# Two heads of a pair on the two halves of the partitions in the delta stage, and x loaded transposed

## Chip, cores and metric

The kernel runs on one core of a Trainium2 chip. The metric is device time in microseconds (us) from the first to the last instruction of the program; one launch computes the whole layer. The engines are named as in the profile: PE is TensorE's matmuls, PEld its weight loads, DVE is VectorE, ACT is ScalarE, POOL is GpSimd, SP is the engine that issues nearly all DMAs.

## What is computed

One layer of a streaming encoder over 4096 prompt frames and 8 running streams of 16 frames, all in float32. The part that the change touches is this, cut from the reference:

```python
xn = rms_norm(h, ln_g)            # h: 4096 x 1024;  xn = h * rsqrt(mean(h*h)) * ln_g
proj = xn @ w_in                  # columns: q,k,v of group A (1536), a, b, z_A, q_B, k_B, v_B, z_B
conv = silu(depthwise_conv4(qkv_a))                       # per channel, along the frames
q, k = l2_norm(q) * 64**-0.5, l2_norm(k)                  # 8 heads of 64
# gated delta rule in blocks of 64 frames; decay, kk, qk, u, w: solved ahead of the scan
def step(s, xs):                                          # 64 blocks, one after the other
    u_c, w_c, qk_c, qd_c, kt_c, gt_c = xs
    v_new = u_c - w_c @ s
    o_c = qd_c @ s + qk_c @ v_new
    s = s * gt_c + kt_c.T @ v_new                         # the state carries the recurrence
    return s, o_c
o_a = rms_norm(o_a, gdn_norm_g) * silu(z_a)
y = x + concat(o_a, o_b) @ w_out, and then a gated embedding on top
```

## The kernel before

The program is a row of stages with a barrier of all engines between them: `project_a`, `project_b`, `delta`, `delta_sample`, `attend_sample`, `attend`, `combine`. Each engine has its own instruction stream, written out by hand; the streams meet at semaphores only, and an engine that waits holds everything behind it in its own stream.

**project_a** makes q, k, v of group A with the channels on the partitions. The work is 16 blocks of 256 frames (the middle one holds the sample tile too), each with 12 groups of 128 channels. Every product is three float32r matmuls (high x high, low x high, high x low; `matmul3`, lines 88 to 90) for each of 8 slices of the contraction, 24 matmuls a group. While block b is multiplied, the tiles of 128 frames of block b+1 are made ready, two of them (33 in all). A tile goes: SP loads x (`load_x`, L276, two buffers), ACT squares and sums (`square`, L442), POOL makes 1/rms (`norm`), ACT scales x in place (`scale`, L446), PE turns it with 8 transposes into two PSUM banks (`transposes`, L560, called after groups 3 and 8), DVE multiplies by ln_g on the way out (`full`, L662), ACT rounds to the high part (`split_hi`, L453), DVE subtracts for the low part (`split_lo`, L668), SP spills the turned tile for project_b (`spill`, L280). In every group ACT takes the product out of PSUM (`a_raw`, L513), DVE does the four taps of the convolution (L682, L685), ACT the SiLU. Keys and queries of the last block are multiplied after groups 0 to 3 (L600), and small steps for the gates are spread over the groups (`gate_steps`). Block b+1 may start when the low part of its last tile is there. The weights are split once at the start: 32 pieces, `hi_part` on ACT, `lo_part` on DVE for even pieces and on POOL for odd ones.

**project_b** reads the spilled tiles and splits its own weights in the same way (ACT L1228, DVE L1314); meanwhile the engines solve the triangular systems and write per-chunk matrices `UQ`, key rows `krow`, `ketr` and query factors `qrow`.

**delta** runs the recurrence: 64 chunks n of 64 frames, two to a tile t of 128 frames. Rows are frames: the even chunk of a tile sits on partitions 0 to 63, the odd one on 64 to 127, and the eight heads lie side by side in the columns. A chunk is a chain through three engines, cut into two halves x of four heads so that they can follow one another:

- PE `keys_state(n, x)` (L1738): keys times state S, into `psS`
- DVE `residual` (L1829): r = value - gain x that, one instruction for each head on 64x64
- PE `solved` (L1757): the solved matrix times r, into `psV`
- ACT `new_values` (L1673): out of PSUM, 64x256 for each half
- PE `new_state` (L1774): scaled keys times new values, into `psD`
- DVE `state` (L1841): S = decayed S + `psD`; then the next chunk's keys_state

Beside it PE does `queries_state` (L1749) and, one chunk late, `outputs(n - 1)` (L1765); ACT does `decayed` (L1693), `out_rows` (L1680), `out_square` (L1686), and `values(t + 1)` (L1664) at the end of odd chunks; DVE does `keys(t + 1)` (L1813) and `out_sums` (L1847); POOL scales the queries (`scaled`, L1624) and norms the outputs. After the even chunk PE turns keys and values of the next tile in one call of eight transposes (`prepare`, L1721 and L1723). Each 64x64 product is two matmul instructions in the profile. Before the first chunk, SP brings `rows` (three kinds of factors, 24 rows), PE turns them in 32 transposes (L1781), and DVE copies them.

Of the kernel before, what the change touches and what calls it, by code (L numbers as in the profile page):

```python
# [31 lines left out]
P = 128  # L32
# [82 lines left out]
def project_a(nc, d, s):  # L115
# [13 lines left out]
    RING, SLOTS = 6, 7  # L129
# [4 lines left out]
    with ExitStack() as stack:  # L134
# [3 lines left out]
        x_raw = [ph.sb(f"a_x{i}", [P, D]) for i in range(2)]  # L138
        squares = ph.sb("a_squares", [P, D], mybir.dt.bfloat16)
        x_full = [ph.sb(f"a_x_full{i}", [P, KT, P]) for i in range(2)]  # L140
# [30 lines left out]
        psT = ph.ps("a_psT", [P, KT * P])  # L171
# [16 lines left out]
        x_in = [ph.sem(f"a_x_in{i}") for i in range(2)]  # L188
# [3 lines left out]
        scaled = ph.sem("a_scaled")  # L192
        xT_ps = ph.sem("a_xT_ps")
# [19 lines left out]
        spilled = [ph.sem(f"a_spilled{i}") for i in range(2)]  # L213
# [48 lines left out]
        def lo_part(eng, m, done):  # L262
            k, a, b = PIECES[m]
            eng.wait_ge(w_hi_ok, m + 1)
            eng.tensor_tensor(w_lo[:, k, a:b], stage[m % SLOTS][:, 0:b - a], w_hi[:, k, a:b].bitcast(F32),
                              ALU.subtract).then_inc(done, 1)
# [4 lines left out]
        def _(sp):  # L271
            def load_x(t):
                if t >= 2:
                    sp.wait_ge(xT_ps, t - 1)
                src = d.x_p[order[t] * P:(order[t] + 1) * P, :] if t != SAMPLE else d.x_s
                sp.dma_start(x_raw[t % 2][:, :], src).then_inc(x_in[t % 2], 16)  # L276

            def spill(t):
                sp.wait_ge(full_ok, t + 1)
                sp.dma_start(d.xT[order[t]], x_full[t % 2][:, :, :]).then_inc(spilled[t % 2], 16)  # L280
# [36 lines left out]
            load_x(0)  # L317
            with nc.allow_non_contiguous_dma(reason="small per-channel constants, once"):
                sp.dma_start(lnT[:, :], d.ln_g.rearrange("(k p) -> p k", p=P)).then_inc(ln_in, 16)
            load_x(1)  # L320
            for m, (k, a, b) in enumerate(PIECES):
# [5 lines left out]
                if m == 5:  # L327
                    with nc.allow_non_contiguous_dma(reason="small per-channel constants, once"):
# [4 lines left out]
                        sp.dma_start(alog[0:HA, :], d.a_log.rearrange("(h o) -> h o", o=1)).then_inc(consts, 16)  # L333
                if m == 16:
                    load_x(2)
                    spill(0)
                if m == 20:
                    load_x(3)
                    spill(1)
            for b in range(BLOCKS):  # L340
# [27 lines left out]
            for i in range(2):  # L368
                sp.wait_ge(stored[i], 16 * (BLOCKS // 2))
                sp.wait_ge(kq_out[i], 32 * 2 * BLOCKS)  # L370
                sp.wait_ge(spilled[i], 16 * ((TILES + 1 - i) // 2))
# [7 lines left out]
        def _(pool):  # L379
# [36 lines left out]

            norm(0)
            norm(1)
            for i in range(HALVES // 2):
                lo_part(pool, 2 * i + 1, w_lo_g)  # L420
            for b in range(BLOCKS):
# [15 lines left out]
        def _(e):  # L437
            def square(t):
                e.wait_ge(x_in[t % 2], 16 * (t // 2 + 1))
                if t:  # L440
                    e.wait_ge(ssq_ok, t)
                e.activation(squares[:, :], x_raw[t % 2][:, :], ACT.Square, accum_out=ssq[:, t % 2:t % 2 + 1]).then_inc(ssq_ok, 1)  # L442

            def scale(t):
                e.wait_ge(rstd_ok, t + 1)
                e.activation(x_raw[t % 2][:, :], x_raw[t % 2][:, :], ACT.Copy, scale=rstd[:, t % 2:t % 2 + 1]).then_inc(scaled, 1)  # L446

            def split_hi(t):
# [4 lines left out]
                e.activation(xT_hi[b % 2][:, :, a * P:(a + 1) * P], x_full[t % 2][:, :, :], ACT.Copy).then_inc(hi_ok, 1)  # L453

            def hi_part(m):
                k, a, b = PIECES[m]
                e.wait_ge(w_in[m % SLOTS], 16 * (m // SLOTS + 1))
                e.activation(w_hi[:, k, a:b], stage[m % SLOTS][:, 0:b - a], ACT.Copy).then_inc(w_hi_ok, 1)
# [19 lines left out]
            square(1)  # L478
            scale(0)
            hi_part(0)  # L480
            hi_part(1)
            scale(1)
            for m in range(2, HALVES):
# [3 lines left out]
                if m == 8:  # L487
# [13 lines left out]
            for b in range(BLOCKS):  # L501
                ahead = list(tiles_of(b + 1))
                for g in range(G):
# [19 lines left out]
                    if ahead:  # L523
                        if g == 0:
                            square(ahead[0])
                        if g == 1:
                            scale(ahead[0])
                        if g == 4:
                            split_hi(ahead[0])
                    if len(ahead) > 1:  # L530
                        if g == 5:
                            square(ahead[1])
                        if g == 6:
                            scale(ahead[1])
                        if g == 9:
                            split_hi(ahead[1])
                    if len(ahead) > 2:
                        if g == 7:
                            square(ahead[2])
                        if g == 9:  # L540
                            scale(ahead[2])
# [10 lines left out]
        def _(pe):  # L552
            pe.wait_ge(filled, 7)

            def transposes(t):
                pe.wait_ge(scaled, t + 1)
                if t:
                    pe.wait_ge(full_ok, t)
                for k in range(KT):
# [3193 lines left out]
```

## Time and profile before

| | us |
|---|---|
| median of 3 runs | 3620.63 (3614.67 to 3621.94) |
| time of the profiled execution | 3616.96 |
| its span | 3615.2 |
| PE busy in it | 3311.5 |
| DVE, ACT, POOL busy | 2440.0, 1519.8, 1348.5 |
| mean granted clock of TensorE | 0.965 of full |

The span is cut into stages by the instructions that belong to each: project_a to 783, project_b to 1721, delta to 2057, the sample stages to 2260, attend to 2760, combine to the end. A matmul is listed from its issue to its modelled end and overlaps the next ones, so the distance from one start to the next, not the listed duration, is what it costs.

### The profile page before, as it was taken

The numbers are of one execution on the slowest core, as the hardware profiler recorded it, in microseconds if no ns is written. First come the engines' busy times: TensorE is split into PE (matmuls) and PEld (weight loads), VectorE is DVE, ScalarE is ACT, GpSimd is POOL, SyncE is SP. The second block draws the span as 40 slices with busy tenths as digits, with TensorE's granted clock in tenths as the row PEclk, the third lists the DMA queues.
The fourth block names the chain that finished last, engine by engine and source line by source line (L and its number), as shares of the span: only waits on it lengthen the run. The fifth ranks groups of instructions, "written<-read, shape, count | busy, mean of one in ns | idle before, by whom it ended". The sixth has DMA issues, their size and how long they took to land. (4 is left out here: it accounts for less than half of the span.)

```text
span 3615.2 us, 68943 instructions
## 1 busy us (share of the span) xinstructions
PE 3311.5 (92%) x26156; PEld 2827.1 (78%) x26156; DVE 2440.0 (67%) x4770; ACT 1519.8 (42%) x2959; POOL 1348.5 (37%) x1561
## 2 busy tenths in 40 slices
PE   7999999969998999999777667999997999999998
PEld 6999899957886888888676544888885788778887
DVE  7777687745997878682465454766666655666765
ACT  5555455533223323211455423666664222344443
POOL 3222222219896836310466610000001233455664
PEclk9999999989999999999799878999998999999999
DMA  5343244344436552523866355222223544322221
GB/s 157 109 112 113 86 118 114 100 146 132 135 104 184 173 152 103 147 79 113 254 212 228 81 146 187 89 74 75 88 74 129 186 155 148 112 76 100 79 105 63
DMA packets 330646, 455.19 MB, mean 126 GB/s; under 512 B 189555, under 2 KB 212371, under 8 KB 325702
## 3 DMA queue, kind: packets, MB, share of 16 engines
q1 hardware_dynamic: 330318, 450.77, 39.5%
q8 instruction: 211, 3.46, 0.4%
q14 instruction: 117, 0.96, 0.1%
HBM read 276.56 MB, written 176.76 MB: 125 GB/s over the span
## 5 line engine op out<-in xcount | busy, mean ns | idle before, releaser
L88 PE MATMUL b_psP<-b_w_hi,b_xT_hi 128*128 128x512 f32 x1320 | 519.2, 393 | 41.2 <-DVE b_xT_lo L1319 24.3
L89 PE MATMUL b_psP<-b_w_lo,b_xT_hi 128*128 128x512 f32 x1320 | 517.1, 392 | 0.0
L90 PE MATMUL b_psP<-b_w_hi,b_xT_lo 128*128 128x512 f32 x1320 | 516.6, 391 | 0.0
L88 PE MATMUL a_psG<-a_xT_hi,a_w_hi 128*128 128x256 f32 (+1 forms) x1536 | 454.0, 296 | 21.1 <-DVE a_xT_lo L668 19.5
L89 PE MATMUL a_psG<-a_xT_lo,a_w_hi 128*128 128x256 f32 (+1 forms) x1536 | 441.5, 287 | 0.0
L90 PE MATMUL a_psG<-a_xT_hi,a_w_lo 128*128 128x256 f32 (+1 forms) x1536 | 441.0, 287 | 0.0
L88 PE MATMUL h_psM<-h_w_hi,h_c_hi 128*128 128x512 f32 x928 | 371.1, 400 | 37.8 <-DVE h_w_lo L3257 16.3
L89 PE MATMUL h_psM<-h_w_lo,h_c_hi 128*128 128x512 f32 x928 | 366.3, 395 | 0.0
L90 PE MATMUL h_psM<-h_w_hi,h_c_lo 128*128 128x512 f32 x928 | 366.1, 394 | 0.0
L3241 POOL TENSOR_TENSOR h_c_lo<-h_c_lo_whole,h_c_hi 128x512 fp32r<-128x512 f32 x162 | 219.2, 1380 | 325.0 <-ACT h_c_hi L3342 325.0
L88 PEld LDWEIGHTS a_psG<-a_xT_hi,a_w_hi 128*128 128x128 f32 x1536 | 295.3, 192 | 42.7 <-DVE a_xT_lo L668 23.5
L88 PEld LDWEIGHTS b_psP<-b_w_hi,b_xT_hi 128*128 128x128 f32 x1320 | 249.8, 189 | 99.7 <-DVE b_xT_lo L1319 48.0
L685 DVE SCALAR_TENSOR_TENSOR a_act<-a_raw,a_taps,a_act 128x256 f32<-128x256 f32 x576 | 289.1, 502 | 20.6
L89 PEld LDWEIGHTS a_psG<-a_xT_lo,a_w_hi 128*128 128x128 f32 x1536 | 295.7, 192 | 0.0
L90 PEld LDWEIGHTS a_psG<-a_xT_hi,a_w_lo 128*128 128x128 f32 x1536 | 295.5, 192 | 0.0
L90 PEld LDWEIGHTS b_psP<-b_w_hi,b_xT_lo 128*128 128x128 f32 x1320 | 249.7, 189 | 52.4
L3540 DVE TENSOR_TENSOR h_acc<-h_acc,h_psM 128x512 f32<-128x512 f32 x322 | 210.0, 682 | 119.7 <-PE h_psM L90 119.6
L89 PEld LDWEIGHTS b_psP<-b_w_lo,b_xT_hi 128*128 128x128 f32 x1320 | 250.1, 189 | 51.4
L408 POOL COPY a_halo<-a_raw 128x3 f32<-128x3 f32 x192 | 74.3, 387 | 503.3 <-ACT a_raw L513 501.9
L2652 DVE CUSTOM_DVE_ANT_0 f_neg<-f_score,f_bias 128x640 f32<-128x640 f32 (+4 forms) x256 | 192.4, 780 | 82.4 <-PE f_score L2552 52.7
L88 PEld LDWEIGHTS h_psM<-h_w_hi,h_c_hi 128*128 128x128 f32 x928 | 177.3, 191 | 80.0 <-issue 33.4
L1282 ACT ACTIVATE b_rows<-b_psP 128x512 f32<-128x512 f32 x99 | 59.3, 599 | 390.6 <-PE b_psP L90 383.4
(378 smaller groups left out, 7375.1 us busy)
## 6 DMA issues: line engine op xcount, KB each, us to landing
rows_b<-b_rows SPq DMA_DIRECT2D x165, 256.0 KB, 2.2
b_x_full<-xT SPq DMA_DIRECT2D x78, 512.0 KB, 4.3
qkvB<-a_act SPq DMA_DIRECT2D x16, 1536.0 KB, 5.4
d_conv_T<-qkvB SPq DMA_DIRECT2D x16, 1536.0 KB, 10.8
xT<-a_x_full SPq DMA_DIRECT2D x33, 512.0 KB, 3.3
out<-h_rows SPq DMA_DIRECT2D x33, 512.0 KB, 2.7
a_x<-in_x_prompt SPq DMA_DIRECT2D x32, 512.0 KB, 4.4
kq<-a_kq SPq DMA_DIRECT2D x128, 128.0 KB, 2.8
```

What stands on the lines that cost most here:

```text
L88: nc.tensor.matmul(out, x_hi, w_hi, start=first, stop=False)
L89: nc.tensor.matmul(out, x_hi, w_lo, start=False, stop=False)
L90: return nc.tensor.matmul(out, x_lo, w_hi, start=False, stop=last)
L408: pool.tensor_copy(halo[:, g, :], x[:, N:]).then_inc(halo_ok, 1)
L685: v.scalar_tensor_tensor(out, x[:, j:j + N], taps[:, j, g:g + 1], out, ALU.mult, ALU.add).then_inc(conv, 1)
L1282: e.activation(rows[u % ROWS][:, :], psP[u % BANKS][:, :], ACT.Copy if seg == V else ACT.Silu).then_inc(taken, 1)
L2652: v.tensor_tensor_reduce(neg[h % 2][:, 0:n], score[h % 2][:, 0:n], bias[:, h, KEYS - n:], -1.0 / ROOT, BIG, ALU.add, ALU.min, low[a.b][:, ...
L3241: eng.tensor_tensor(c_lo[i][:, :, :], c_raw[i][:, :, :], c_hi[i][:, :, :].bitcast(F32), ALU.subtract)\
L3540: v.tensor_tensor(there, there, psM[u % BANKS][:, :], op).then_inc(folded, 1)
```

## The change

**project_a.** x comes twice: as before (one buffer now, for the squares alone) and transposed, from a second input that the host lays out (`load_xT`, three buffers of `x_full`). ACT's `scale` and PE's eight transposes of a tile are gone. PE turns 1/rms of the tile, spread over 128 columns, with one transpose (`spread`, into `psB`), and DVE multiplies the transposed tile by it in place. ln_g goes into the weights: ACT's `hi_part` scales (even pieces in one instruction, odd ones in two), DVE's `lo_part` becomes a scalar_tensor_tensor, POOL scales `w_ab`. **project_b** loads ln_g too and scales its weights in the same two instructions; the columns of z_A come from a copy ordered by halves.

**delta.** The two heads of a pair now sit on the two halves of the partitions (even heads 0 to 63, odd heads 64 to 127), the same frames on both, and the chunks lie side by side in the columns. So every product has its operands and its result on the same half, `residual` is two instructions of 128x64 for each x instead of four of 64x64, and `new_values` and `out_rows` are 128x128 and 128x256. `psS`, `psV` and `psD` of one x share one PSUM bank. Turning is cut into four calls of two transposes; keys and values are then moved onto the halves by two instructions of 64x256 a chunk on DVE (`keys`) and on ACT (`values`). The query factors are no longer broadcast by DMA and multiplied on POOL: PE spreads them with four matmuls a tile (8 rows to 128 x 128, `spread_scales`) and DVE multiplies (`scaled`). za, mixed and UQ are moved in two DMAs each; the factor rows take 12 DMAs and 64 transposes. The order on PE changes: both halves of `outputs` stand ahead of both halves of `new_state`. `delta_sample` and `combine` only read and write in the new order of heads.

The core of the diff:

```diff
 # project_a
+            def load_xT(t):
+                if t >= XBUFS:
+                    sp.wait_ge(spilled[t % XBUFS], 16 * (t // XBUFS))
+                    sp.wait_ge(lo_ok, t - XBUFS + 1)
+                    sp.wait_ge(ab_ok, t - XBUFS + 1)
+                sp.dma_start(x_full[t % XBUFS][:, :, :], src.rearrange("p (k n) -> p k n", k=KT)).then_inc(xT_in[t % XBUFS], 16)
-                    if t + 2 < TILES:
-                        load_x(t + 2)
+                    if t + 1 < TILES:
+                        load_x(t + 1)
+                        load_xT(t + 1)
                     spill(t)
-                for k in range(KT):
-                    last = nc.tensor.transpose(psT[:, k * P:(k + 1) * P], x_raw[t % 2][:, k * P:(k + 1) * P], ident[:, :])
+                nc.tensor.transpose(psB[:, 0:P], rstd[:, a:a + 1].to_broadcast([P, P]), ident[:, :]).then_inc(rstd_ps, 1)
-                v.tensor_tensor(x_full[t % 2][:, :, :], psT[:, :].rearrange("p (k n) -> p k n", k=KT),
-                                lnT[:, :].unsqueeze(2).to_broadcast([P, KT, P]), ALU.mult).then_inc(full_ok, 1)
+                v.tensor_tensor(x[:, :, :], x[:, :, :], psB[:, 0:P].unsqueeze(1).to_broadcast([P, KT, P]), ALU.mult)\
+                    .then_inc(full_ok, 1)
...
 # delta, DVE
-                    for a in range(2):
-                        for e in range(2):
-                            op = v.scalar_tensor_tensor(r[c, cols], psS[x][c, e, a, :], key_gain[c, t, h:h + 1], vt[t % 2][c, cols],
-                                                        ALU.mult, ALU.add)
+                    for a in range(2):
+                        p = 2 * x + a
+                        op = v.scalar_tensor_tensor(r[c][:, p, :], psS[x][:, a, :], key_gain[:, n, p:p + 1], vt[t % 2][:, c, p, :],
+                                                    ALU.mult, ALU.add)
...
 # delta, PE
             for n in range(NCH):
+                ahead = n // 2 + 1
                 keys_state(n, 0)
                 keys_state(n, 1)
                 queries_state(n, 0)
+                queries_state(n, 1)
+                if ahead < NT:
+                    (turn_values, turn_keys)[n % 2](ahead, n % 2)
                 solved(n, 0)
-                queries_state(n, 1)
                 solved(n, 1)
+                if ahead < NT and n % 2 == 0:
+                    turn_values(ahead, 1)
+                if ahead + 1 < NT and n % 2 == 1:
+                    spread_scales(ahead + 1)
                 if n:
                     outputs(n - 1, 0)
+                    outputs(n - 1, 1)
                 new_state(n, 0)
-                if n:
-                    outputs(n - 1, 1)
                 new_state(n, 1)
-                if n % 2 == 0 and n // 2 + 1 < NT:
-                    prepare(n // 2 + 1)
+                if ahead < NT and n % 2 == 0:
+                    turn_keys(ahead, 0)
...
 # delta, DVE, a chunk
                 residual(n)
-                if n % 2 == 1 and t + 1 < NT:
-                    keys(t + 1)
+                if n + 1 < NCH:
+                    keys(n + 1)
                 state(n)
-                if n % 2 == 0 and t:
+                if n % 2 == 1 and t:
                     out_sums(t - 1)
+                if n % 2 == 0 and t and t + 1 < NT:
+                    scaled(t + 1)
```

## Rows read from the trace of the kernel before

**Rows 1.** The page: busy time of each engine over the span.
```profile
PE 3311.5 (92%) x26156; PEld 2827.1 (78%) x26156; DVE 2440.0 (67%) x4770; ACT 1519.8 (42%) x2959; POOL 1348.5 (37%) x1561
```

**Rows 2.** Windows: length, busy us of PE, PEld, DVE, ACT, POOL, clock, DMA, GB/s.
```profile
26.00:755.00 729.00, 710.91 (x6480) 671.77 (x6480) 554.98 (x1079) 387.04 (x732) 184.85 (x472) 0.99 0.37 107
...
1740.00:2057.00 317.00, 253.59 (x5368) 230.37 (x5368) 187.09 (x703) 182.67 (x512) 205.06 (x187) 0.96 0.63 203
...
1750.00:1760.00 10.00, 9.49 (x132) 8.95 (x130) 3.37 (x14) 5.05 (x14) 1.27 (x1) 0.50 1.04 330
```

**Rows 3.** Timeline of PE in project_a: start us, us, engine, line, instruction.
```profile
309.16 1.09 PE L560 MATMUL a_psT<-a_ident,a_x 128*128 128x128 f32 x8
310.00 0.36 PE L88 MATMUL a_psG<-a_xT_hi,a_w_hi 128*128 128x256 f32 x1
```

**Rows 4.** Timeline of DVE and PE at the end of a block.
```profile
323.47 0.35 DVE L682 TENSOR_SCALAR a_act<-a_raw,a_taps 128x256 f32<-128x256 f32 x1 [1.70 <-ACT a_raw L513]
...
335.46 1.22 DVE L668 TENSOR_TENSOR a_xT_lo<-a_x_full,a_xT_hi 128x1024 fp32r<-128x1024 f32 x1
...
336.74 0.39 PE L88 MATMUL a_psG<-a_xT_hi,a_w_hi 128*128 128x256 f32 x1 [0.51 <-DVE a_xT_lo L668]
```

**Rows 5.** Timeline of the delta loop, one pair of chunks.
```profile
1882.47 0.29 DVE L1841 TENSOR_TENSOR d_S<-d_sgt,d_psC 128x128 f32<-128x128 f32 x1 [1.15 <-PE d_psC L1774]
...
1884.85 1.72 DVE L1829 SCALAR_TENSOR_TENSOR d_r<-d_psC,d_key_gain,d_vt 64x64 f32<-64x64 f32 x8
...
1885.81 0.50 PE L1757 MATMUL d_psC<-d_r,d_UQ 64*64 64x64 f32 x5 [0.97 <-DVE d_r L1829]
...
1886.52 0.38 ACT L1673 ACTIVATE d_vn<-d_psC 64x256 f32<-64x256 f32 x1 [1.47 <-PE d_psC L1757]
...
1886.63 0.50 PE L1757 MATMUL d_psC<-d_r,d_UQ 64*64 64x64 f32 x5
...
1887.20 0.27 PE L1774 MATMUL d_psC<-d_vn,d_kt 64*64 64x64 f32 x2
...
1887.72 0.29 DVE L1841 TENSOR_TENSOR d_S<-d_sgt,d_psC 128x128 f32<-128x128 f32 x1 [0.43 <-PE d_psC L1774]
...
1889.26 1.62 DVE L1829 SCALAR_TENSOR_TENSOR d_r<-d_psC,d_key_gain,d_vt 64x64 f32<-64x64 f32 x8 [0.70 <-ACT d_vt L1664]
...
1892.02 0.29 DVE L1841 TENSOR_TENSOR d_S<-d_sgt,d_psC 128x128 f32<-128x128 f32 x1 [1.15 <-PE d_psC L1774]
...
1892.18 0.34 PE L1774 MATMUL d_psC<-d_vn,d_kt 64*64 64x64 f32 x6
...
1892.45 0.66 PE L1721 MATMUL d_psA<-d_ident,d_conv_T 128*128 128x128 f32 x4
...
1893.47 0.68 PE L1738 MATMUL d_psC<-d_S,d_conv_T 64*64 64x64 f32 x16
```

**Rows 6.** Timeline of SP and ACT in project_a: a load of x, and a square.
```profile
312.07 0.62 SPq L276 DMA_DIRECT2D a_x<-in_x_prompt  x1
...
316.70 1.05 ACT L442 ACTIVATE a_squares<-a_x 128x1024 bf16<-128x1024 f32 x1
```

**Rows 7.** DMA issues: KB each, median us to landing.
```profile
a_x<-in_x_prompt SPq DMA_DIRECT2D x32, 512.0 KB, 4.4
```

**Rows 8.** Lines of ACT in project_a, with and without a scale from memory.
```profile
L446 ACT ACTIVATE a_x<-a_x,a_rstd 128x1024 f32<-128x1024 f32 x33 | 37.6, 1139 | 0.0
...
L453 ACT ACTIVATE a_xT_hi<-a_x_full 128x1024 fp32r<-128x1024 f32 x33 | 34.7, 1053 | 15.2 <-DVE a_x_full L662 15.2
```

**Rows 9.** Lines of DVE in delta.
```profile
L1813 DVE TENSOR_TENSOR d_kt<-d_psA,d_scal 128x512 f32<-128x512 f32 x32 | 22.1, 692 | 5.3 <-PE d_psB L1723 4.4
```

**Rows 10.** Timeline of PE before the first chunk of delta.
```profile
1730.50 1.87 PE L1781 MATMUL d_psA<-d_ident,d_rows 24*128 24x24 f32 x16 [12.79 <-DMA d_rows<-ssqT]
...
1738.06 1.09 PE L1721 MATMUL d_psA<-d_ident,d_conv_T 128*128 128x128 f32 x4 [3.98 <-DMA d_UQ<-UQ]
...
1739.93 1.12 PE L1738 MATMUL d_psC<-d_S,d_conv_T 64*64 64x64 f32 x16
```

More of the change, by code:

```diff
@@ L610, in query_sums @@
                 last.then_inc(rows_ps, 1)
-            transposes(0)
-            transposes(1)
+            spread(0)
+            spread(1)
             for b in range(BLOCKS):
@@ L1121, in _ @@
             load_x(0)
+            with nc.allow_non_contiguous_dma(reason="small per-channel constants, once"):
+                sp.dma_start(lnT[:, :], d.ln_g.rearrange("(k p) -> p k", p=P)).then_inc(ln_in, 16)
             for k in range(KT):
@@ L1576, in store @@
             def store(t):
                 sp.wait_ge(g_out, t + 1)
-                sp.dma_start(d.mixed[t * P:(t + 1) * P, 0:W], out[t % 2][:, :]).then_inc(stored[t % 2], 16)
-            for n in range(NCH // 16):
-                for first, src in ((0, d.ketr), (2 * H, d.krow)):
-                    there = rows[first:first + H, n // 2 * 32 * C:(n // 2 + 1) * 32 * C]
-                    sp.dma_start(there.rearrange("h (c e i) -> h c e i", e=2, i=C)[:, :, n % 2, :],
-                                 src[16 * n:16 * (n + 1)].rearrange("c h i -> h c i")).then_inc(rows_in, 16)
@@ L1585, in _ @@
-            sp.dma_start(rows[H:2 * H, :], d.ssqT).then_inc(rows_in, 16)
+                for e in range(2):
+                    here = out[t % 2][e * C:(e + 1) * C, :].rearrange("i (c w) -> i c w", c=2)
+                    sp.dma_start(tokens(d.mixed, t, e), here).then_inc(stored[t % 2], 16)
+            for e in range(2):
+                for first, src in ((0, d.ketr), (2 * PAIRS, d.krow)):
+                    for x in range(2):
+                        sp.dma_start(rows[first:first + PAIRS, x::2, e, :],
+                                     src[x * NCH // 2:(x + 1) * NCH // 2, e * PAIRS:(e + 1) * PAIRS].rearrange("n a i -> a n i"))                            .then_inc(rows_in, 16)
@@ L1775, in new_state @@
+                for p, a, rows_e in half_heads(x):
+                    last = nc.tensor.matmul(psD[x][rows_e, a, :], kt[t % 2][rows_e, c, p, :], vn[c][rows_e, p, :], start=True, stop=True)
                 last.then_inc(t_ds, 1)
[L1777 to L1781 removed]
+            pe.wait_ge(rows_in, 16 * 10)
@@ L1782, in _ @@
+            for n in range(NCH):
+                to = (psA, psB)[n // NT]
+                at = n % NT * 3 * PAIRS
+                last = nc.tensor.transpose(to[:, at:at + 3 * PAIRS], rows[:, n, :, :].rearrange("k e i -> k (e i)"),
+                                           ident[0:3 * PAIRS, 0:3 * PAIRS])
             last.then_inc(t_rows, 1)
             pe.wait_ge(v_scal, 2)
-            prepare(0)
+            for c in range(2):
+                turn_values(0, c)
+            for c in range(2):
+                turn_keys(0, c)
```

419 lines of the change are left out of this document (236 added, 183 removed).

## The prediction

> **What bounds the kernel now.** I read the page first: PE is busy for 92% of the span and every other engine for 67% or less [rows 1]. But that is an average over stages, so next the windows by stage [rows 2]. In project_a PE is busy for 711 of 729 us: this stage is as long as what PE issues. In the delta loop PE is busy for 254 of 317 us while nothing else is near full: this stage is a chain. Then the timeline of each. In project_a the eight transposes of a tile start at 309.16 and the next group at 310.00 [rows 3], so a tile's turning costs PE 0.84 us, 0.105 for each transpose. At the end of a block PE stands 0.51 us because the low part of the last tile ends late; DVE had worked without a pause from 323.47 until that part was done at 336.68 [rows 4]. So a second chain lies close behind PE there.
>
> In delta the loop repeats every 9.55 us (first half of S at 1882.47 and again at 1892.02, two chunks) [rows 5]. I call R the start of `residual` and S0 the start of the state's first half. R to S0 is 2.87 in the odd chunk (1884.85 to 1887.72) and 2.76 in the even one (1889.26 to 1892.02). S0 to R is 2.38 before the odd chunk, where PE turns the next tile first and DVE sums the outputs, and 1.54 before the even one, where R waits for ACT's copy of the values (0.70 in the row). PE runs at 1.2 GHz (granted 0.50) at 1750 to 1760, after PE had stood idle between the stages, and over the whole loop at 0.96 [rows 2].
>
> **project_a, part by part.** Eight transposes become one: 0.84 becomes about 0.15 (one transpose and the change of weights), 0.69 less for each of 33 tiles, 31 of them inside the blocks: 21.4 us. ACT's scale of 1.14 us [rows 8] goes too. It lies beside PE, but in group 6 it stands ahead of the evacuation for which DVE's closing chain starts, so that chain starts earlier as well, by about 1.1 plus the 0.69 of the first transpose call, and PE's wait at the boundary shouldn't grow. DVE's multiply keeps its size, 128x1024 with one operand from PSUM. ln_g in the weights: a scale from memory costs ACT 0.09 on 1024 columns (1139 against 1053 ns) [rows 8]; the 16 odd pieces pay a second ACT instruction, about 0.5 each for 384 columns, beside PE but for the start. Half of them fall into block 0, where x(3) is now also loaded later, behind the weights. The first product should start about where it does, since the turning is out of its chain and more ACT work is in it. I put 1 us for all that, between 2 less and 5 more. SP: the load of x that follows the key stores is now for the square in the same block instead of a later one. Issued at 312.07 plus 0.62 [rows 6] plus 4.4 to landing [rows 7] gives 317.1; the square would start at 316.7 less 0.69 [rows 6]. ACT then waits 1.1 us, which it has to spare in group 5 or 6. Tiles of transposed x land half a block before they are needed. Sum: 20 less.
>
> **project_b.** Eight scaled weight pieces before the first products end, 8 x 0.09 less what hides behind their DMAs, and one more small DMA ahead of them, about 0.6 as for x [rows 6]: 1.2 more, between 0 and 4. In its loop PE covers the scaling; if it did not, 24 pieces x 0.09 would be 2 us.
>
> **Ahead of the chunks.** 32 transposes of 24 rows become 64 of 12: 16 of them take 1.87 listed, less the last one's tail of 0.28, so 0.106 each [rows 10], 3.4 more. Before the first chunk PE now also spreads two tiles: 16 instructions of 128 columns. At full clock I take 0.105 each as for a transpose [rows 3]; here PE runs at 1.2 GHz [rows 2], so 0.21, 3.4 in all, and DVE multiplies behind it. Before, PE also stood idle there for UQ until 1738.06 [rows 10], behind the query factors' DMAs that are gone, which covers 3 of the 4 us of that wait. With 0.7 for DVE's multiply, from 1739.93 the first key product moves to about 1744.5: 4.5 more, between 2 and 8.
>
> **The loop.** R to S0, new. `residual` has eight instructions in 1.72, 0.215 each; half of them are ready for PE after 0.96 (1884.85 to 1885.81) [rows 5]. Now it has four in all, so after that 0.96 both halves are ready, not only the first. Then PE: `solved` of the second half. Eight instructions on one quarter of the array reach their reader after 0.71 (1885.81 to 1886.52), eight that alternate between two quarters after 0.52 (1887.20 to 1887.72) [rows 5]; the 0.2 between them is eight instructions at about 0.056 in one queue against four in each of two. So a call now issues in 0.22 where `solved` and `outputs` took 0.45. But `outputs` of chunk n - 1 used to run on the other chunk's quarter, beside `solved`; now it shares the quarters and stands ahead of `new_state`: two calls, 0.45. In the even chunk two transposes stand there too, 0.21. The spread in the odd chunk is eight instructions, 0.84.
>
> Each of these also leaves the 64x64 form and comes back. The trace shows both: the last of the six state products from 1892.18 issues near 1892.30 and the first transpose at 1892.45, 0.15; and eight transposes until the next key product take 1.02 (1892.45 to 1893.47), 0.18 more than the 0.84 of rows 3 [rows 3, 5]. I add 0.33. The Trainium skill, "TensorEngine Tiling (Array Packing)", Key Properties, says that changing the tiling mode drains TensorE. By the trace such a drain costs 0.15 to 0.18; with none the pair would be 0.66 shorter.
>
> Even: 0.96 + 0.22 + 0.54 + 0.45 + 0.52 = 2.69. Odd: 0.96 + 0.22 + 1.17 + 0.45 + 0.52 = 3.32. ACT's copy of the new values, 0.38 before [rows 5], has 128 columns less, about 0.27 by the 0.9 ns a column of L453 (1053 for 1024) [rows 8], and isn't late on this path.
>
> S0 to R, new. DVE does both state halves (0.25 each in sequence), then `out_sums` in odd chunks and `scaled` in even ones, each the size of the 692 ns of L1813 [rows 9]: 1.2. PE's own way (0.29 for the add and the 0.52 of a call for the key product) is about 0.85, so DVE sets it. The turning is out of the way, and the copy of the values is made a chunk earlier. Two times 1.2 against 2.38 + 1.54. New pair: 2.69 + 3.32 + 2.4 = 8.4, 1.15 less than 9.55; 31 of 32 pairs: 35.6 less. What is hidden: DVE's keys (two of about 0.42, by the 692 ns for 512 columns) lie between the residual's end and S0, ready long before; ACT was busy for 183 of 317 us [rows 2], 5.5 a pair, and its new copies weigh about what its old ones did. If switches cost nothing and the spread ran beside something the pair would be 7.5; if each switch cost double and ACT's order bit, 9.1. DMA moves less (the broadcast factors go), in smaller runs. The sample stages get 256-byte runs for z_A and mixed: 0.5 more.
>
> Sum: -20 + 1.2 + 4.5 - 35.6 + 0.5 = -49.4. From the profiled execution's 3616.96 that is 3567.6; the median of the runs lies 3.7 above that execution, inside their own spread. I predict **3568 us**, own range 3550 to 3585.
>
> **Rivals.** *project_a gives it back.* DVE's closing chain of 13.2 us [rows 4] isn't started earlier, or ACT's wait for x is passed on. Then each boundary eats the 0.69 of a call or of both: 10 to 20 us lost, 3578 to 3588, I say 3583. For it: PE already waits there. Against: the scale ahead of that chain is gone. Chance 0.12.
>
> *The loop gains half.* ACT's order after an even chunk (out_rows, two value copies, squares, then the decays) makes the new values late, or the switches cost double: pair 9.0, 18 lost, 3586. Chance 0.13.
>
> *The halves take turns (slower).* Now both halves' products write one PSUM bank at the same time, on its two halves of partitions. In the trace products from two row halves (keys, queries) go to separate banks, so no row shows this. If the two queues took turns, every call issues in 0.45 and PE becomes the bound: keys 0.9, queries 0.9, turning 0.54, solved 0.9, again 0.54 or 1.17, outputs 0.9, 0.74 to S0, 0.34 on: 5.8 and 6.4, pair 12.2. That is 2.65 more for 31 pairs: 82, with the rest (-13.8) 3685. It decides from a call above about 0.28, where the pair passes 9.55. The skill, same page, Gotcha 1, says that different row tiles cannot access the same PSUM bank simultaneously; by that rule this is what happens. Against it: the products of new_state wrote both halves of one bank at full rate, though from one row half. Chance 0.08.
>
> *Better*: a pair of 7.8 or less and a boundary without a wait, 3545. Chance 0.12. *Clock*: PE at 1.2 GHz through the loop, as at 1750 [rows 2]: a pair near 11.3, 3640. Against it: PE has no longer gaps than before. Chance 0.03. The forecast keeps 0.52.
>
> **Chances and range.** Runs of this kernel differ by 0.2%, 7 us, and nothing smaller can be told from no change. The first, second and better cases all end below 3613; both losses together, 3601, do too. Faster 0.86, the same 0.04 (losses at their upper ends together), slower 0.10. The 0.8 range takes the better case's and both losing cases' middle: 3538 to 3606.
>
> **What would show it.** In project_a 24 matmuls a group as before, one L-transpose of about 0.15 a tile, the distance from block start to block start shorter by 1.4. In delta the distance between every second S0 at 8.4, key and solved calls of eight instructions at 0.22 to 0.26, R set by DVE's sum or scale, a spread of about 0.85 ahead of outputs in odd chunks. Wrong would be: a loop period above 9, DVE waiting at R for PE (turns), a granted clock of 0.5 inside the loop, PE waiting at block boundaries for over 1.5 us, or ACT waiting for x.

## The result, and the profile of the changed kernel

The changed kernel takes 3592.74 us (median of 4 runs, 3590.76 to 3594.14) where the kernel before takes 3620.93. The ratio is 0.9928, with a 95% interval of 0.9916 to 0.9940; measured once more on another chip it is 0.9926 (0.9908 to 0.9944). So the change is worth 26 to 28 us. The forecast was 52.6, half of which didn't come. The time lies inside the range of 3538 to 3606.

The page of the changed kernel, busy time of each engine: as a whole nothing seems to have moved [rows 1].

```profile
PE 3313.3 (92%) x26213; PEld 2808.1 (78%) x26213; DVE 2426.5 (68%) x4646; ACT 1507.9 (42%) x3038; POOL 1311.8 (37%) x1530
```

The windows of the changed kernel say more (columns as in [rows 2]): project_a, delta's loop, and the loop's first 33 us.

```profile
26.00:737.00 711.00, 691.81 (x6279) 651.86 (x6279) 556.25 (x1079) 366.37 (x715) 184.24 (x474) 0.99 0.45 133
...
1742.00:2026.00 284.00, 269.36 (x5611) 227.23 (x5610) 173.64 (x573) 185.00 (x600) 162.24 (x153) 0.95 0.71 190
...
1743.00:1776.00 33.00, 26.79 (x452) 22.20 (x448) 13.87 (x48) 14.24 (x46) 5.39 (x5) 0.77 1.00 206
```

project_a lasts 711 us for 729. In the loop PE is now busy for 269 of 284 us, for 254 of 317 before: the chain has become a stage that PE nearly fills. In the loop's first 33 us PE is idle for 6 of them at a clock of 0.77, and the DMA engines have not a moment free.

Going by marks in both traces, the profiled executions compare as follows (before, after, difference, forecast):

```
start of project_b's products    783.4    764.8   -18.6  (-18.8)
first instruction of delta      1721.8   1703.0   -18.8  (-18.8)
from it to the first key product  18.1     39.4   +21.3  ( +4.5)
from there to the last new state 313.7    281.7   -32.0  (-35.6)
to the sample stage's first PE    22.8     25.3    +2.5  ( +0.5)
the rest                        1538.8   1543.0    +4.2  (  0  )
```

The sum is 22.9 (spans 3615.2 and 3592.3). The missing time stands in one line above all, the entry of delta. Its timeline in the changed kernel, SP's issues and PE:

```profile
1703.74 0.73 SPq L1619 DMA_DIRECT2D d_rows<-ketr  x2
...
1709.89 2.78 SPq L1622 DMA_DIRECT2D d_rows<-ssqT  x2
...
1722.82 3.56 PE L1823 MATMUL d_psA<-d_ident,d_rows 12*128 12x12 f32 x32 [24.04 <-DMA d_rows<-ssqT]
...
1735.72 1.09 PE L1747 MATMUL d_psB<-d_ident,d_conv_T 128*128 128x128 f32 x4 [5.93 <-DMA d_UQ<-UQ]
...
1737.59 2.07 PE L1765 MATMUL d_psQ<-d_q_rows,d_spread 8*128 8x128 f32 x8
...
1740.44 2.07 PE L1765 MATMUL d_psQ<-d_q_rows,d_spread 8*128 8x128 f32 x8 [0.78 <-DVE d_Qd L1881]
```

The factor rows are there 19.8 us after the stage's start (1722.8 less 1703.0); before it was 8.7 (1730.5 [rows 10] less 1721.8). That is 11.1. Their 64 transposes take 3.4 more. PE then waits 5.93 for UQ for 3.98 [rows 10], 2.0 more. From turning to the first key product it is 6.7 for 1.9, 4.8 more, for two spreads and VectorE between them. Together 21.3.

The loop's timeline, one pair of chunks of the changed kernel:

```profile
1877.51 0.52 DVE L1905 TENSOR_TENSOR d_S<-d_sgt,d_psC 128x128 f32<-128x128 f32 x2 [0.93 <-PE d_psC L1816]
...
1878.55 0.85 DVE L1893 SCALAR_TENSOR_TENSOR d_r<-d_psC,d_key_gain,d_vt 128x64 f32<-128x64 f32 x4
...
1879.44 0.68 PE L1798 MATMUL d_psC<-d_r,d_UQ 64*64 64x64 f32 x16
...
1880.06 1.15 PE L1765 MATMUL d_psQ<-d_q_rows,d_spread 8*128 8x128 f32 x8
1881.14 0.68 PE L1806 MATMUL d_psO<-d_vn,d_UQ 64*64 64x64 f32 x16
1881.65 0.63 PE L1816 MATMUL d_psC<-d_vn,d_kt 64*64 64x64 f32 x16
...
1882.10 0.52 DVE L1905 TENSOR_TENSOR d_S<-d_sgt,d_psC 128x128 f32<-128x128 f32 x2 [1.68 <-PE d_psC L1816]
...
1883.14 0.85 DVE L1893 SCALAR_TENSOR_TENSOR d_r<-d_psC,d_key_gain,d_vt 128x64 f32<-128x64 f32 x4
...
1885.83 0.52 DVE L1905 TENSOR_TENSOR d_S<-d_sgt,d_psC 128x128 f32<-128x128 f32 x2 [0.93 <-PE d_psC L1816]
```

R to S0 is 3.55 in the odd chunk (1878.55 to 1882.10) and 2.69 in the even one, S0 to R 1.04 each time: a pair of 8.32 for 9.55 [rows 5]. Sixteen matmul instructions (eight products of 64x64) are issued in 0.51 (1881.14 to 1881.65), though the two row halves write one PSUM bank.

So 31 steady pairs would give 38 us, and 32 came. The waits of PE inside the loop, 1742 to 2026, show where 6 went (us in total, times, longest):

```profile
PE d_psC L1798 <- issue: 4.5, 1, 4.5
...
PE d_psQ L1765 <- issue: 2.7, 2, 1.7
PE d_psC L1816 <- issue: 1.6, 2, 1.0
```

Here "issue" is time in which PE waited for no semaphore: 8.8 us, for 2.9 in the kernel before. The longest, in the timeline, cuts a run of sixteen matmul instructions after the fourth:

```profile
1756.65 0.52 DVE L1905 TENSOR_TENSOR d_S<-d_sgt,d_psC 128x128 f32<-128x128 f32 x2 [1.27 <-PE d_psC L1816]
...
1758.59 0.33 PE L1798 MATMUL d_psC<-d_r,d_UQ 64*64 64x64 f32 x4
...
1763.43 0.90 PE L1798 MATMUL d_psC<-d_r,d_UQ 64*64 64x64 f32 x12 [4.51 <-issue]
...
1766.26 1.12 PE L1806 MATMUL d_psO<-d_vn,d_UQ 64*64 64x64 f32 x16
...
1767.85 0.71 DVE L1905 TENSOR_TENSOR d_S<-d_sgt,d_psC 128x128 f32<-128x128 f32 x2 [8.29 <-PE d_psC L1816]
```

Sixteen instructions are listed with 1.12 behind the pause and 0.68 elsewhere: PE's clock has fallen to 1.2 GHz (granted 0.50 from 1763 to 1768). S0 to S0 is 11.20 here for 4.59, so a pause of 4.5 cost 6.6.

### The profile page after: what moved, and what is told of

Its sections match the earlier page's. It is cut to its first block and busy times, and to the rows that moved or that the text cites. A ratio compares the mean times of both kernels' runs of the same rounds, so it can differ in the third digit from the quotient of the medians.

```text
span 3592.3 us, 69141 instructions
## 1 busy us (share of the span) xinstructions
PE 3313.3 (92%) x26213; PEld 2808.1 (78%) x26213; DVE 2426.5 (68%) x4646; ACT 1507.9 (42%) x3038; POOL 1311.8 (37%) x1530
## 3 DMA queue, kind: packets, MB, share of 16 engines
q8 instruction: 211, 3.46, 0.4%
## 5 line engine op out<-in xcount | busy, mean ns | idle before, releaser
L88 PE MATMUL a_psG<-a_xT_hi,a_w_hi 128*128 128x256 f32 (+1 forms) x1536 | 455.2, 296 | 18.4 <-DVE a_xT_lo L684 14.2
L701 DVE SCALAR_TENSOR_TENSOR a_act<-a_raw,a_taps,a_act 128x256 f32<-128x256 f32 x576 | 307.5, 534 | 20.5
## 6 DMA issues: line engine op xcount, KB each, us to landing
d_conv_T<-qkvB SPq DMA_DIRECT2D x16, 1536.0 KB, 10.3
```

What stands on the lines that cost most here:

```text
L88: nc.tensor.matmul(out, x_hi, w_hi, start=first, stop=False)
L701: v.scalar_tensor_tensor(out, x[:, j:j + N], taps[:, j, g:g + 1], out, ALU.mult, ALU.add).then_inc(conv, 1)
```

## The experiments

The kernel before was timed on the same chip beside each group of kernels; its median was 3614.7, 3618.9, 3617.5 and 3621.5 us in the four groups. Differences below are worked out from the ratios; by its ratio the changed kernel stands at 26.5 less. Two kernels of different groups can't be told apart by less than some 5 us.

### 1 and 2. The new project_a with the old delta

The edit keeps the hunks of project_a and `scale=lnT[:, k:k + 1]` in project_b, and takes delta, the scratch layouts and the last stage from the kernel before.

> The kernel before with the new project_a and the weights of project_b scaled by ln_g, the delta stage left as before. Theory: the first half of the change gives what the two traces show at project_b's end, 18.8 us, and the rest of the kernel doesn't notice it: 3602, ratio 0.995. Rival: part of the gain is taken back further on, or comes only because delta's operands changed: under 12 us, above 3609.

Measured: 3607.07, ratio 0.9978 (0.9968 to 0.9989), 8 us less. In its profile delta begins at 1704.0. The mean granted clock of its 12 runs was 0.962, of the kernel before 0.965. Since 8 doesn't fit 18.8, the kernel was run once more:

> The kernel before with the new project_a once more on another chip. The first measurement gave 8 us (4 to 12) though delta began 18 us earlier in the profile. If a part of the gain is regularly paid back at the low clock: again 6 to 11 us, mean clock 0.003 below that of before. If that was chance: 14 to 19 us.

Measured: 3605.22, ratio 0.9953 (0.9939 to 0.9968), 17 us less; delta begins at 1703.3. The second run fits the traces and the first doesn't; they lie 9 us apart, and why the first gave so little stays open. That a part is regularly paid back is not shown. The changed kernel's second measurement (0.9926) was made to ask the same: expected were 22 to 30 us less at a mean clock of 0.962 or below if a part is paid back, and it gave 27 less at 0.960 for 0.965. But the changed kernel also pauses more in its loop (7.6 us there), which lowers the clock without any payback, so that this decides nothing.

### 3. Factor rows with the chunk on the partition

```
-rows = [3 * PAIRS, NCH, 2, C]      # 12 partitions; each load goes to 4
+rows = [NCH, 3, PAIRS, 2, C]       # 64 partitions
-for n in range(NCH):  transpose(.., rows[:, n], ..)          # 64 transposes of 12 rows
+for k in range(12):   transpose(.., rows[:, k // 4, k % 4])  # 12 transposes of 64 rows
```

> The changed kernel with the factor rows loaded with the chunk on the partition (64 partitions) in place of the pair (4 partitions), and 12 transposes for 64. Theory A: a load onto 4 partitions uses a quarter of the DMA engines, and what is queued behind it (first keys, first UQ) waits for these engines: the rows land some 10 us earlier, the first key product starts 24 to 28 us after the stage's start for 39.4, the kernel is 12 to 16 us shorter than the changed one (about 3579). Rival B: the first tiles' 2 MB and the low clock set the start: the rows land earlier, the first key product moves only by the transposes, under 5 us, and the kernel by as much.

Measured: 3578.25, ratio 0.9899 (0.9882 to 0.9916), 36.5 us less than before and 10 less than the changed kernel. Its timeline:

```profile
1707.69 0.31 DVE L1859 MEMSET d_S<- 128x128 f32 x2 [12.26 <-PEq L56]
...
1714.74 1.08 PE L1821 MATMUL d_psA<-d_ident,d_rows 64*128 64x64 f32 x8 [11.27 <-DMA d_rows<-ssqT]
...
1725.74 1.09 PE L1746 MATMUL d_psB<-d_ident,d_conv_T 128*128 128x128 f32 x4 [9.49 <-DMA d_UQ<-UQ]
...
1732.46 1.12 PE L1779 MATMUL d_psC<-d_S,d_conv_T 64*64 64x64 f32 x16
```

The rows are there after 7.0 us for 19.8, the first key product starts after 24.8 for 39.4: theory A's numbers for the entry. The kernel gained 10 where 12 to 16 were expected. The edit does two things: the rows are 12.8 us earlier and their transposes 5.5 us shorter (12 for 64), while PE's wait for UQ grows by 3.6, to 9.49.

### 4. The kernel before, with its row loads cut onto 4 partitions

```
-        sp.dma_start(rows[first:first + H, ..], src[16 * n:16 * (n + 1)] ..)
+        for z in (0, 4):
+            sp.dma_start(rows[first + z:first + z + 4, ..], src[16 * n:16 * (n + 1), z:z + 4] ..)
```

> The kernel before with nothing changed but its nine loads of factor rows cut in two by heads, so that each goes to 4 partitions for 8, the same bytes in the same runs (ssqT in two halves as well). Theory A: the rows land 6 to 10 us later than the 8.7 us after the stage's start, and the first key product with them: 5 to 9 us slower, about 3627. Rival B: only the 9 more issues at 0.33 us on SP count, 3 us or less.

Measured: ratio 1.0013 (1.0002 to 1.0024), 4.7 us more. Rows after 12.5 for 8.7, first key product 22.0 for 18.1. The rows' 3.8 more lie between the theories (6 to 10, and 3 for the issues alone) and decide nothing.

### 5. Only the order of the loads

```
+load_raw(0); load(0)          # the first tile
 ... the ten loads of factor rows, two of q_rows ...
-for t in range(BUFS):
+for t in range(1, BUFS):
```

> The changed kernel with only the order of SP's loads changed: keys, values, UQ and z_A of the first tile ahead of the factor rows, which stay on 4 partitions. Theory A (a load onto 4 partitions fills 4 of 16 engines, and each load behind it waits for those): the first tile's loads land by about 15 us after the stage's start for 32.7, and the turning then starts when the factor rows are there and turned, at 27 to 30; the first key product 3 to 6 us earlier than 39.4. Rival B (bytes and the low clock): the rows are later by what was put ahead of them, 8 us or more, and the first key product is not earlier than 39.

Measured: ratio 0.9918 (0.9902 to 0.9934), not told apart from the changed kernel's. In its timeline PE waits for the rows until 1732.87, 27.8 us after the start at 1705.1, and the first key product starts after 42.6. The rows are 8 us later by what was put ahead of them: theory A failed here, rival B held. The wait for UQ was not what held the stage; the rows' own time was.

### 6 and 7. The same additional runs of 256 bytes, on 4 and on 64 partitions

Both kernels issue the loads of factor rows once more ahead of the real ones, into a tile `extra` that nothing reads.

> The changed kernel with each of the ten factor-row loads issued once more ahead of the others, into a tile that nothing reads: 12 partitions, 3072 runs of 256 bytes for 1536. Theory A' (four engines carry them, 384 runs each, at the 48 ns a run that 18.3 us for 384 give): the rows land 18 us later, 38 us after the stage's start for 19.8, first key product at 55 to 58, the kernel 15 to 18 us slower than the changed one, ratio 0.997. Rival: the time is the fixed cost of ten DMAs or waits at its two ends: under 8 us.

> The kernel with chunk rows with its eight factor-row loads issued once more into a tile that nothing reads: the same 1536 more runs of 256 bytes, on 64 partitions. Theory A': sixteen engines carry them, 96 more runs each at 48 to 62 ns, 5 to 6 us more: rows at 12 to 13 us after the start for 7.0, the kernel under 6 us slower than chunk rows alone. Rival: the runs cost the same wherever they go (one issuing queue): 18 us more.

Measured: on 4 partitions a ratio of 0.9954 (0.9937 to 0.9971), 10 us slower than the changed kernel: rows after 30.1 for 19.8, first key product 49.7 for 39.4. On 64 partitions a ratio of 0.9899 (0.9880 to 0.9917), as with chunk rows alone: rows after 11.5 for 7.0, first key product 28.5 for 24.8.

```profile
1737.82 3.56 PE L1832 MATMUL d_psA<-d_ident,d_rows 12*128 12x12 f32 x32 [34.38 <-DMA d_rows<-ssqT]
1719.44 1.08 PE L1829 MATMUL d_psA<-d_ident,d_rows 64*128 64x64 f32 x8 [15.76 <-DMA d_rows<-ssqT]
```

The first line is the kernel with 4 partitions, whose stage starts at 1707.7, the second the one with 64, from 1707.9. The same 1536 runs cost 10.3 us on few partitions and 4.5 on many. So the destination matters, but by 2.3 to 1 and not by the 4 to 1 that was expected, and if four engines carry them, at 27 ns a run on each instead of 48. SP takes nearly as long to issue the additional loads, 8.7 us for ten on 4 partitions and 4.7 for eight on 64; whether its issues are slow by themselves or held up by busy engines is not separated.

### 8. Loads 4 tiles ahead in place of 6

```
-BUFS = 6: six tiles are loaded before the first chunk, tile t + 6 when tile t is done
+DEPTH = 4: four tiles, and tile t + 4 when tile t is done
```

> The kernel with chunk rows, loading 4 tiles ahead in place of 6. Theory F (PE's pauses without a semaphore in the loop, 8.8 us in the changed kernel for 2.9 before, are instructions that come late because the data loads fill the DMA engines): with less loaded ahead the pauses in the first 30 us of the loop fall under 3 us with their stretches at 1.2 GHz, 4 to 8 us less than with chunk rows alone. Rival G: the pauses stay, within 3 us; or tiles land late and it is slower.

Measured, on top of the chunk rows: 3572.62, ratio 0.9871 (0.9855 to 0.9887), 10 us less than chunk rows alone. PE's pauses in the loop are 4.6 us for 8.6. In the first 30 us of it they are 1.3 us, which looks like the sign that was expected (under 3), but with chunk rows alone they were 2.8 already. On the changed kernel:

> The changed kernel with the loads 4 tiles ahead in place of 6, nothing else. Theory F: the pauses of PE without a semaphore early in the loop (7.6 and 8.8 us in two profiles) and the stretches at 1.2 GHz behind them go, first key product to last state near 269 us for 279: 8 us less than the changed kernel, about 3585 where the kernel before has 3619. Rival G: what paid with the chunk rows was an earlier start, here under 3 us.

Measured: 3578.72, ratio 0.9895 (0.9878 to 0.9911), 11 us less than the changed kernel. First key product to last new state is 267.3 for 281.7. Its window of the loop's start and its waits in the loop:

```profile
1742.00:1776.00 34.00, 32.94 (x650) 27.37 (x648) 19.93 (x67) 20.38 (x67) 10.78 (x10) 0.94 0.82 194
```

```profile
PE d_psC L1818 <- issue: 1.3, 3, 0.5
PE d_psO L1808 <- issue: 0.5, 2, 0.3
```

PE is busy for 32.9 of 34 us at a clock of 0.94 and its pauses are 1.8 us for 8.8. And on the kernel before:

> The kernel before with its loads 4 tiles ahead in place of 6. Theory F: its loop leaves the DMA engines more time (pair 9.55) and lost 8 us to pauses and slow pairs at its start and in three places, most of it while the first loads ran: 3 to 5 us less, so that about half of what pacing gives the changed kernel is not owed to the change. Rival: nothing within 2 us, the pauses are the change's own.

Measured: ratio 0.9993 (0.9984 to 1.0003), 2.5 us less and not told from nothing. So most of the 11 is owed to the change.

### 9. No spread in the loop

`spread_scales` is called for the first two tiles only; the other tiles are scaled by the second one's factors, so this leaves out a part of the computation.

> The changed kernel without the spreading of the query factors by TensorE inside the loop (tiles 2 to 31 are scaled with the factors of the second tile; VectorE's multiply stays). The forecast priced it at 1.17 us a pair of chunks, 0.84 and two changes of the tiling: pair 8.32 to 7.15, 30 pairs, 35 us less. Rival: VectorE or ScalarE sets the odd chunk as soon as it is gone, pair 7.8 or more, 15 us or less.

Measured: ratio 0.9871 (0.9853 to 0.9889), 20 us less than the changed kernel. The steady pair, by VectorE's first state half:

```profile
1880.09 0.52 DVE L1903 TENSOR_TENSOR d_S<-d_sgt,d_psC 128x128 f32<-128x128 f32 x2 [0.93 <-PE d_psC L1816]
1883.45 0.52 DVE L1903 TENSOR_TENSOR d_S<-d_sgt,d_psC 128x128 f32<-128x128 f32 x2 [0.46 <-PE d_psC L1816]
1887.18 0.52 DVE L1903 TENSOR_TENSOR d_S<-d_sgt,d_psC 128x128 f32<-128x128 f32 x2 [0.93 <-PE d_psC L1816]
```

7.09 for 8.32, so the spread costs 1.23 a pair; priced were 1.17. But PE's pauses grew to 16.5 us: a still faster loop pauses more, and the kernel keeps 20 of 37.

### 10. The spread beside the turning

In odd chunks `spread_scales(ahead + 1)` is called right behind `turn_keys`, ahead of `solved`.

> The changed kernel with the spread of the odd chunks placed right behind the turning of two tiles of keys, ahead of the solved product, so that PE changes its tiling once less a pair and back. Theory D (PE sets the loop, a change and back is 0.33): pair 8.32 to 8.0, 10 us less. Rival E: the solved product is 0.84 later, the new values with it, and nothing is left to cover ScalarE's copy: pair 8.5 to 9.1, 6 to 25 us more.

Measured: ratio 0.9918 (0.9903 to 0.9933), 3 us less than the changed kernel and not told from it. Its pair is steady at 8.17 (4.44 and 3.73), 0.15 less: half of theory D's 0.33 a pair, and none of rival E.

### 11 to 13. The entry reordered, and the parts together

> The kernel with the chunk on the partition for its factor rows, and the stage's start in another order: keys, values and UQ of the first tile loaded ahead of the factor rows, the first spread ahead of the turning, the second spread (with VectorE's scaling) moved into the first chunk. Theory A (after the few-engine loads are gone, the first key product waits for what stands ahead of the first UQ in SP's queue, and for two spreads at 1.2 GHz): first key product 17 to 20 us after the stage's start for 24.8, 5 to 7 us less than the kernel with chunk rows alone, about 3572. Rival B: the low clock and the landing times set it, under 2 us.

Measured: 3573.06, ratio 0.9868 (0.9851 to 0.9886), 11 us less than chunk rows alone, where 5 to 7 were expected, though the first key product moved only from 24.8 to 22.0 and not to 17 to 20. In the profiles another 5.4 us come from the stretch between it and the sample stage, in which PE paused for 5.6 us instead of 8.6.

> Chunk rows, the first tile's loads first, the first spread ahead of the turning and the second in the first chunk, 4 tiles ahead, and the spread behind the turning in odd chunks. By the parts, each against the changed kernel (ratio 0.9926): chunk rows and order 21 us, pacing 8 to 10, the spread 3 to 4.6, together 32 to 36: about 3560 where the kernel before has 3619, ratio 0.984. Rival: pacing and order remove the same waits, 24 us, ratio 0.986.

Measured: 3565.79, ratio 0.9855 (0.9841 to 0.9870): the rival's number. Its rows arrive 16.5 us after the start, since the first tile's loads stand ahead of them.

> The kernel of the joined parts with the factor rows first again and the first tile behind them. Its rows landed 16.5 us after the stage's start behind the first tile's loads, and with chunk rows alone 7.0 us after: first key product at 19 to 21 for 21.9, 1 to 3 us less than the joined parts, ratio 0.985; and over 0.986 if the joined parts' 0.9855 was the low side of chance.

Measured: 3561.45, ratio 0.9843 (0.9822 to 0.9863), the fastest kernel of the study, 57 us less than before and 30 less than the changed kernel. Its timeline:

```profile
1709.07 1.08 PE L1832 MATMUL d_psA<-d_ident,d_rows 64*128 64x64 f32 x8 [11.14 <-DMA d_rows<-ssqT]
...
1712.76 2.07 PE L1775 MATMUL d_psQ<-d_q_rows,d_spread 8*128 8x128 f32 x8 [2.19 <-DMA d_q_rows<-qrow]
...
1722.13 1.12 PE L1790 MATMUL d_psC<-d_S,d_conv_T 64*64 64x64 f32 x16
```

From the start at 1702.1 the rows take 7.0 and the first key product 20.0. Against the kernel of the joined parts it is 4 us, inside both intervals.

## Why the prediction was off

**project_a and project_b: right.** 20 less and 1.2 more; the marks show 18.6 to 18.8 less. The one transpose that is left costs PE 0.16, where 0.15 was taken; products follow one another at 0.12, here the second starts 0.28 after the transpose:

```profile
304.00 0.32 PE L581 MATMUL a_psB<-a_ident,a_rstd 128*128 128x128 f32 x1
304.07 0.36 PE L88 MATMUL a_psG<-a_xT_hi,a_w_hi 128*128 128x256 f32 x1
304.28 0.28 PE L89 MATMUL a_psG<-a_xT_lo,a_w_hi 128*128 128x256 f32 x1
304.39 0.29 PE L90 MATMUL a_psG<-a_xT_hi,a_w_lo 128*128 128x256 f32 x1
```

PE's wait for the low part fell from 19.5 to 14.2 us in all, as the removed scale ahead of that chain suggested. By the traces the rival in which project_a gives it back is out; alone and timed, the part gave 8 and 17 us, and the 8 is not explained.

**Ahead of the chunks: the step that failed.** Its 4.5 had a term for the 3.4 of more transposes (3.4 measured), one for the spreads and VectorE (4.1; 4.8 measured), and 3 us back from PE's wait for UQ, "behind the query factors' DMAs that are gone, which covers 3 of the 4 us of that wait". That wait grew by 2.0. And there was no term at all for the loads of the factor rows, which came 11.1 us later, the largest number of the stage. The change moves them from 8 destination partitions to 4; the diff shows it, `rows[first:first + PAIRS, ..]` for `rows[first:first + H, ..]`, and SP's rows as well: a pair of these issues now takes up to 2.8 us where one took 0.3. It also cuts `ssqT`, which came as eight long rows, into 512 runs of 256 bytes, 1536 runs in all for 1024 (packets under 512 bytes in the entry: 2257 for 1257, with 512 of the query factors among them). Experiment 3 gives the time back (12.8 us of rows, 14.6 of the first key product, 10 of the kernel), with the same 1536 runs. Experiments 6 and 7 show that additional runs cost 2.3 times as much on few partitions. The Trainium skill, "DMA: Bandwidth & Descriptors", section "Why a DMA increments its semaphore by 16 and not by 1", says that a DMA uses as many engines, up to 16, as divide the slowest dimension of both its sides. By that rule a load onto 4 partitions has 4 engines and one onto 64 has 16. The trace agrees in direction. Its row of the DMA engines' busy tenths, from 1702 to 1723 in slices of 0.525 us, shows two or three tenths (once four) from 1706.7 to 1715.6, while only these loads and the query factors' run,

```profile
DMA  0000146633333433332322321526752918699997
```

but the measured price of the doubled runs differs by 2.3 and not by 4. In the kernel before the cut from 8 to 4 partitions cost 3.8 us, of which SP's nine additional issues explain 3; it left `ssqT` in long rows, so that the 512 more runs are not in it. At the price of experiment 6 (10.3 us for 1536) they would be 3.4 us, an estimate; no kernel tested them alone. So how the 11.1 divides between fewer partitions, more runs and SP's issue stays open.

**The loop: right in its period, wrong in its sum.** The pair was forecast at 8.4 and is 8.32; even chunk 2.69 as worked out, odd chunk 3.55 for 3.32 (the first half of `solved` doesn't go ahead of the second as I had it; all sixteen instructions are issued in 0.62 with the change of tiling), S0 to R 1.04 for 1.2. That 8.4 came so close is in part luck, since the 0.23 too little and the 0.32 too much cancel. The spread was priced at 1.17 and is 1.23. The change of tiling was priced at 0.33 for leaving and coming back; experiment 10 saved one such excursion a pair and gained 0.15. "The halves take turns" is refuted by the calls at 0.25 for eight instructions. The Trainium skill, "TensorEngine Tiling (Array Packing)", Gotcha 1, says that row tiles can't use one bank at the same time; the trace doesn't agree for this form, 64x64 tiles on the diagonal, as far as the rate of issue tells: 0.032 us an instruction, for about 0.056 on one quarter. What the sum lacked was a term for PE's pauses, which rose from 2.9 to 8.8 us and drew stretches at 1.2 GHz after them. They grow as the pair gets shorter (2.9 us at 9.55, 8.8 at 8.32, 16.5 at 7.09). Experiment 8 shows that loading less far ahead gives 11 us here, 2.5 and uncertain before, and that the changed kernel's pauses go with it (1.8 for 8.8). It is not their whole cause: the joined kernel, loaded 4 tiles ahead, paused for 6.8 us.

That what comes late are PE's own instructions I had only argued, from pauses that no semaphore explains; the traces show it. The page of the changed kernel lists 211 DMAs of 16 KB as instructions, each for some 124 matmuls with their weight loads (26213 / 211):

```profile
q8 instruction: 211, 3.46, 0.4%
```

That they are PE's is read from their size (3.46 MB are 66 bytes for each of its matmuls and weight loads) and from what follows. In all 18 traces, between 1742 and 2028, the timelines list 92 pauses of PE without a semaphore, and each of them ends 1.2 to 1.7 us after one of these DMAs has landed. The longest of the changed kernel ends at 1763.43; its DMA ran from 1760.57 to 1761.84, 10.3 us after the start of the one before it. Loaded 4 tiles ahead, the changed kernel gets them 5.5 and 5.7 us apart there and hardly pauses. At its 650 matmuls in 34 us 124 last 6.5 us, an estimate, so that one every 10 us is too few.

Full DMA engines alone don't make PE pause. In the kernel before they are as full at the loop's start, and no pause is listed in its first 30 us:

```profile
1740.00:1776.00 36.00, 31.61 (x518) 28.64 (x519) 18.91 (x73) 17.68 (x51) 16.43 (x16) 0.72 1.04 316
```

Its instruction DMAs start 9.0 and 8.1 us apart there, but at 518 matmuls in 36 us 124 last 8.6 us. So the slower loop can live with that spacing, and the faster one can't. That it is the data loads on the same engines that hold the instruction DMAs back is argued, from experiment 8 alone.

**The rest.** The sample stage's first work begins 2.5 us later after the last state, for 0.5; what made it later was not looked for. The remaining 4.2 us are within what profiles of one kernel differ by: the same stretch is 1506 to 1509 us long from the sample stage's first state products in three profiles with the old project_a, 1505 to 1516 in fifteen with the new one.

Two side sums of the prediction are wrong; the forecast doesn't hang on them. With a pair of 11.3 the clock rival comes to 3568 + 31 x 2.9 = 3658 and not 3640. With no price for the switches and the spread hidden, its own terms give a pair of 8.4 - 0.66 - 0.84 = 6.9 where it says 7.5, and it names no other bound.

That 3593 lies inside the range of 3538 to 3606 is luck. Its upper part stood for lost time at project_a's boundaries and for a pair of 9.0, and neither came; the loss came from a stage that was priced at 2 to 8 us and took 21.

Taken together: the profiled executions differ by 22.9 us where the sum said 49.4. Of the missing 26.5 the entry is 16.8, the loop 3.6, the passage to the sample stage 2.0 and the rest 4.2. The first two are mended by measured kernels: chunk rows give 10 us, loading 4 tiles ahead gives 10 to 11 (more than the loop's 3.6, since the loop's start also gets faster than it was before). Chunk rows with either of the other two edits bring the same change to 47 or 48 us, all of them together to 52 to 57.

## What to carry to other kernels

When a layout moves to fewer partitions, price the loads that fill it, not only the instructions that read it: count the short runs, the old and the new ones, and the partitions that share them, and look at how long SP takes to issue them. After a stage has got faster, ask what it now outruns; here loading less far ahead was worth as much as the better layout of the factor rows. A pause of PE that no semaphore explains can be its own instructions: look for the instruction DMA that lands just ahead of its end. And a short stretch at 1.2 GHz in PE's clock was here the mark of such a pause.

## What the runs showed that I had not expected

- Loads of 1536 runs of 256 bytes were there after 7.0 us on 64 partitions and 19.8 on 4.
- All 92 pauses of PE without a semaphore end 1.2 to 1.7 us after an instruction DMA of 16 KB has landed.
- Two diagonal 64x64 tiles write one PSUM bank at 0.032 us a matmul instruction (16 in 0.51).
- Loading 6 tiles ahead instead of 4 cost 11 us with a pair of 8.32; with one of 9.55 it cost 2.5, which can't be told from nothing.
- One kernel timed against the kernel before on two chips gave ratios of 0.9978 (0.9968 to 0.9989) and 0.9953 (0.9939 to 0.9968), intervals that only touch: an interval from one chip is not the whole uncertainty.
